# Which operand stays in TensorE in a compression of keys and values

## The reference

```
flat = blocks + pe                      # [n_cmp, 2 groups, 32 * 64]
k_cmp = gelu(flat @ w1) @ w2            # w1: 2048 x 256, w2: 256 x 64
k_cmp = rope(k_cmp at the block's end)  # keys only
```

## Time and profile before

| | |
|---|---|
| median of three timed runs | 3112.48 us |
| profiled execution | 3098.76 us, span 3097.4 us |
| TensorE matmul busy | 2260.3 us, 73% |
| TensorE weight load busy | 1385.4 us, 45% |
| VectorE busy | 1795.0 us, 58% |
| ScalarE busy | 462.6 us, 15% |
| GpSimd busy | 1330.2 us, 43% |
| DMA | 829.56 MB, 268 GB/s on average |
| mean granted TensorE clock | 0.802 of 2.4 GHz |

### The profile page before, as it was taken

How to read it: one execution, slowest core, us unless ns; L and a number is a source line. 1 busy time by engine, 2 the same in 40 slices (tenths; PEclk the granted TensorE clock), 3 DMA queues, 4 the chain that set the end, 5 groups by cost and what they waited for, 6 DMA issues and landing times. The chain is left out here.

```text
span 3097.4 us, 24710 instructions
## 1 busy us (share of the span) xinstructions
PE 2260.3 (73%) x8222; PEld 1385.4 (45%) x8222; DVE 1795.0 (58%) x3876; ACT 462.6 (15%) x1305; POOL 1330.2 (43%) x1041
## 2 busy tenths in 40 slices
PE   5997982046692594777684578979957687969988
PEld 3545861023442472533343336758425343437543
DVE  1512017988878777777567996774656954223300
ACT  1201000001210100111100332012000321013310
POOL 0000001376767677666668763674665533100000
PEclk9886996568695696898785557989977699986999
DMA  3310431589889899978889876999998879942466
GB/s 124 131 63 33 150 114 57 172 301 389 311 302 355 308 402 369 376 291 319 327 285 389 310 258 229 391 374 400 359 367 328 281 259 392 343 148 90 147 248 223
DMA packets 291758, 829.56 MB, mean 268 GB/s; under 512 B 23568, under 2 KB 30016, under 8 KB 290864
## 3 DMA queue, kind: packets, MB, share of 16 engines
q0 software_dynamic: 148464, 539.99, 47.8%
q1 hardware_dynamic: 139872, 283.19, 25.3%
q10 hardware_dynamic: 3296, 4.80, 0.4%
HBM read 825.81 MB, written 2.10 MB: 267 GB/s over the span
## 5 line engine op out<-in xcount | busy, mean ns | idle before, releaser
L314 POOL DMA_INDIRECT picks_rows<-peer_u_dram,expert x512 | 701.8, 1371 | 858.9 <-DVE expert L1475 521.0
L314 POOL DMA_INDIRECT picks_rows<-peer_v_dram,expert x512 | 620.8, 1213 | 502.8 <-DVE h L380 346.5
L374 DVE CUSTOM_DVE_ANT_0 picks_rows<-picks_rows,xn 128x1024 f32<-128x1024 f32 x512 | 613.4, 1223 | 168.7 <-DMA picks_rows<-peer_u_dram,expert 148.7
L380 DVE SCALAR_TENSOR_TENSOR h<-picks_rows,picks_weight,h 128x1024 f32<-128x1024 f32 x416 | 533.4, 1282 | 153.5 <-DMA picks_rows<-peer_v_dram,expert 82.8
L465 PE MATMUL psum<-weight_ring,hnT 128*128 128x512 f32 (+4 forms) x576 | 236.4, 572 | 23.9 <-DMA weight_ring<-w_in_dram 11.9
L1763 PE MATMUL psum<-weight_ring,aT 128*128 128x512 f32 x512 | 220.8, 593 | 2.9 <-ACT aT L2070 1.4
L403 PE MATMUL psum<-picks_rows,picks_diag 128*128 128x512 f32 x384 | 172.0, 607 | 27.4 <-ACT picks_diag L332 24.3
L465 PEld LDWEIGHTS psum<-weight_ring,hnT 128*128 128x128 f32 (+1 forms) x576 | 105.8, 186 | 153.1 <-issue 137.4
L656 PE MATMUL psum<-identity_sb,n_scaled 128*128 128x128 f32 (+1 forms) x104 | 23.9, 409 | 183.6 <-DVE n_scaled L640 183.6
L1763 PEld LDWEIGHTS psum<-weight_ring,aT 128*128 128x128 f32 x512 | 97.0, 190 | 125.1 <-issue 120.5
L876 PE MATMUL psum<-identity_sb,na_probs 128*128 128x128 f32 (+2 forms) x384 | 92.5, 360 | 72.3 <-DVE na_probs L962 56.2
(11 more groups left out here) (353 smaller groups left out, 3193.4 us busy)
## 6 DMA issues: line engine op xcount, KB each, us to landing
weight_ring<-w_ff_dram SPq DMA_DIRECT2D x48, 2048.0 KB, 10.9
weight_ring<-w_in_dram SPq DMA_DIRECT2D x44, 2048.0 KB, 14.2
weight_ring<-w_proj_nsa_dram SPq DMA_DIRECT2D x6, 2048.0 KB, 8.5
weight_ring<-w_out_dram SPq DMA_DIRECT2D x6, 2048.0 KB, 14.6
weight_ring<-w_ret_out_dram SPq DMA_DIRECT2D x4, 2048.0 KB, 7.8
weight_ring<-w_mix_out_dram SPq DMA_DIRECT2D x4, 2048.0 KB, 18.7
weight_ring<-w_peer_q_dram SPq DMA_DIRECT2D x4, 2048.0 KB, 13.4
picks_rows<-peer_u_dram,expert POOLq DMA_INDIRECT x512, 7.5
```

The source lines that it names most:

```text
L314: pool.indirect_dma_start(out=self.rows[:, n % GATHERS, :], out_offset=None, in_=table, in_offset=bass.IndirectOffsetOnAxis(ap=self.expert ...
L374: ins = nc.vector.tensor_tensor_reduce(out=row, in0=row, in1=self.x[t], scale=1.0, scalar=0.0, op0=ALU.mult, op1=ALU.add, accum_out=self.d ...
L380: ins = nc.vector.scalar_tensor_tensor(out=h, in0=row, scalar=self.weight[:, t % 2, k:k + 1], in1=h, op0=ALU.mult, op1=ALU.add)
```

## The change

`compress_stage` keeps the blocks in TensorE and moves the weights. For each l, all 32 columns of both groups (64 with a step of 16) are loaded, and the slab's 256 columns of that l move through. The result is 64 blocks by 256 hidden units in one bank, with one product group per slab. Gelu is applied to it (64x256). Two transposes then turn it, ScalarE copies the 128x128 that come out to `hidden`, and the w2 products follow as before. As all 32 columns are read in all runs, also those not yet written, a new stage clears `kc` once, right behind the table loads.

```
-        two += [("ck1", a["w_ck1"], 2), ("cv1", a["w_cv1"], 2)]
+        two += [("ck1", a["w_ck1"], 1), ("cv1", a["w_cv1"], 1)]
...
+    both = NG * S // CMP_STRIDE
...
-        hidden = sb("hidden", [P, 2, 2, NG * n])
+        by_block, hidden = sb("by_block", [both, 2, CMP_HID]), sb("hidden", [P, 2, 2, both])
...
+                blocks = kc[:, x].rearrange("p g (n l) -> p (g n) l", l=CMP_STRIDE)
+                for l in range(CMP_STRIDE):
+                    mm = nc.tensor.matmul(g.psum[0:both, 2 * x, 0:CMP_HID], blocks[:, :, l], w1[:, l, :], start=(l == 0),
+                                          stop=(l == CMP_STRIDE - 1))
+                mm.then_inc(g.w.products_done, 1)
+            for x in range(2):
+                pe.wait_ge(*s_hidden.after(x + 1))
                 for j in range(2):
-                    for l in range(CMP_STRIDE):
-                        rhs = kc[:, x, :, :].rearrange("p g (n l) -> p g n l", l=CMP_STRIDE)[:, :, 0:n, l]
-                        mm = nc.tensor.matmul(g.psum[:, 2 * x + j, 0:NG * n].rearrange("p (g n) -> p g n", g=NG),
-                                              w1[:, l, P * j:P * j + P], rhs, start=(l == 0), stop=(l == CMP_STRIDE - 1))
-                    mm.then_inc(g.w.products_done, 1)
-                    g.picks.add(pe, 2 * x + j + 1)
+                    mm = nc.tensor.transpose(g.psum[:, 2 * x + 1, both * j:both * j + both], by_block[:, x, P * j:P * j + P],
+                                             g.identity[0:both, 0:both])
+                mm.then_inc(s_flipped.sem, 1)
             for x in range(2):
-                pe.wait_ge(*s_hidden.after(2 * x + 2))
+                pe.wait_ge(*s_flat.after(x + 1))
                 for grp in range(NG):
                     for j in range(2):
                         mm = nc.tensor.matmul(g.psum[0:n, 4 + x, HD * grp:HD * grp + HD],
-                                              hidden[:, x, j, n * grp:n * grp + n], w2[:, x, j, :],
+                                              hidden[:, x, j, both // NG * grp:both // NG * grp + n], w2[:, x, j, :],
                                               start=(j == 0), stop=(j == 1))
...
-                for j in range(2):
-                    act.wait_ge(g.w.products_done, g.w.product(name, j))
-                    nc.scalar.activation(hidden[:, x, j, :], g.psum[:, 2 * x + j, 0:NG * n],
-                                         ACT.Gelu_apprx_tanh).then_inc(s_hidden.sem, 1)
+                act.wait_ge(g.w.products_done, g.w.product(name, 0))
+                nc.scalar.activation(by_block[:, x, :], g.psum[0:both, 2 * x, 0:CMP_HID], ACT.Gelu_apprx_tanh).then_inc(s_hidden.sem, 1)
                 g.picks.activate(act, 2 * x + 2)
+            for x in range(2):
+                act.wait_ge(*s_flipped.after(x + 1))
+                nc.scalar.copy(hidden[:, x].rearrange("p j n -> p (j n)"), g.psum[:, 2 * x + 1, 0:2 * both]).then_inc(s_flat.sem, 1)
...
+def clear_stage(g, name, tensor):
+
+    signal = g.named(name)
+    g.open(None, 1)
+    g.begin(g.nc.vector)
+    g.nc.vector.memset(tensor, 0.0).then_inc(signal.sem, 1)
+    signal.count += 1
+    g.ended["dve"] = signal.after(0)
...
+            clear_stage(g, "blocks_cleared", kc[:])
```

More of the change, by code:

```diff
@@ L1552, in compress_stage @@
     nc = g.nc
+    both = NG * S // CMP_STRIDE
     sig = lambda name: g.named(f"compress_{name}")
-    s_hidden, s_out, s_link, s_roped, s_turned = (sig(x) for x in ("hidden", "out", "link", "roped", "turned"))
+    s_hidden, s_flipped, s_flat, s_out, s_link, s_roped, s_turned = (
+        sig(x) for x in ("hidden", "flipped", "flat", "out", "link", "roped", "turned"))
     names = [("ck1", "second", run), ("cv1", "second", run)]
@@ L1623, in compress_stage @@
         vector(nc.vector)
-    s_hidden.count += 4
+    for signal in (s_hidden, s_flipped, s_flat):
+        signal.count += 2
     s_out.count += 2
@@ L1627, in compress_stage @@
     s_turned.count += 1
-    g.ended["pe"], g.ended["act"], g.ended["dve"] = s_turned.after(0), s_hidden.after(0), s_link.after(0)
+    g.ended["pe"], g.ended["act"], g.ended["dve"] = s_turned.after(0), s_flat.after(0), s_link.after(0)
 def pool_stage(g, tag, uT, tokens, inv_count, w_pool, pool_scale, ypT):
```

## The result

| | before | after |
|---|---|---|
| median | 3106.73 us (22 runs, 3093.57 to 3132.85 and one of 3519.11, which the ratio leaves out) | 3088.01 us (22 runs, 3073.15 to 3111.05) |
| ratio after/before | | 0.9942, 95% interval 0.9926 to 0.9958 |
| profiled execution | 3098.76 us, span 3097.4 | 3074.43 us, span 3073.1 |
| mean granted clock | 0.802 | 0.817 |

The kernel got 0.4 to 0.7% faster. The forecast of 3101.9 us was 13.9 us too high, and the range (from 3089) missed the time by 1 us. Repeated later, the changed kernel gave ratios of 0.9967 and 0.9969.

A forecast was written before the change was run, and what follows sets the result against it. Of three second-wave compression stages (runs 0, 1, 2), only run 2 was taken as bound by TensorE's narrow, low-clock products. Its stage gains 10.6 us (26.5 to 15.9), other parts 0: 3112.5 - 10.6 = 3101.9 us, range 3089 to 3113.

The forecast's parts named there:

- part 6: Turns and attention behind run 2's stage: clock falls in the tail, 0 gained; 8.5 us if it held.
- the base of the sum: Timed median before taken as 3112.5 us, 13.7 above the profiled execution; less 10.6 gives 3101.9.
- What bounds the kernel: Second wave's compression: TensorE carries run 2 (token tile 3), 26.47 us to VectorE's copy; other work ends runs 0 and 1.
- part 4: Runs 0 and 1: TensorE saves some 11 us in each but waits longer for picks; gain 0, upper bound 0.5.
- part 3: Compression slabs given back after one product group, with 1.6 us of cover in run 2; cost 0, upper bound 3.2 us.
- part 1: Run 2's first products: 64 records of 256 columns at 0.2155 us, 13.8 us against 25.34; upper bound 0.31 a record.
- (b): Run 2's products: strided weight load not hidden, 0.263 to 0.31 us a record, gain 4.5 to 7.6, about 3106.5; chance 0.09.
- (c): Run 2's products: 64 weight columns lose the clock, 0.427 us a record, 3.3 us slower, 3115.8; chance 0.06.
- part 2: Behind run 2's products: gelu wait and transposes add 1.0 us; stage 15.9 us against 26.5, gain 10.6; bounds 0.6 and 2.0.
- part 5: Clear behind the last selection: 128x2048 VectorE memset of 2.2 us, off the path, cost 0; without cover 2.3 us.
- signs that the prediction named: Run 2's following turns: clock 0.50 under the forecast, 1.00 under rival (a); also product pace and VectorE's copy at 16 us.
- rival (a): Clock holds through run 2's tail: 10.6 + 8.5 = 19.1 us gained, 3093.4; chance 0.27.

The follow-up runs named there:

- 124 columns side by side: Kernel before, with run 2's (token tile 3) products each moving 124 adjacent columns, wrong blocks; 128 records in 14.5 us, 296.2 us to the end.
- fillers: Changed kernel plus unread identity products in TensorE's waits in run 2 (token tile 3): 3077.70 and 3091.03 us, ratios 0.9929 and 0.9961 to before.
- 124 at the step: Kernel before, run 2 moving 124 columns at a 64-byte step: 62 read twice (3095.60 us, ratio 0.9991) or 124 different (310.3 us to the end).
- with the clear: Kernel before with only the clear of kc added: 3109.04 us, ratio 1.0002 to before.
- with run 2 as before: Kernel before with the clear and the new compression in runs 0 and 1 only, the old one in run 2: 3110.02 us, ratio 1.0007.
- side by side: Kernel before, with run 2's products each moving 62 adjacent columns, wrong blocks; 128 records in 25.4 us, 309.7 us to the end.

## Why the prediction was wrong

Two steps failed: the clock behind the stage, put at no gain (part 6), and the base of the sum, taken from three runs. The stage itself was forecast rightly.

*What bounds the kernel; runs 0 and 1 (part 4); slabs (part 3).* Right. Run 2 alone pays, with 86.2 and 48.3 us against 85.4 and 48.5 in the others. In run 2 no DMA ended a wait of the products: loads and matmuls have one idle gap each, ahead of the first.

```profile
L1576 PE MATMUL psum<-weight_ring,kc_sb x64: 379/379/454, 2776.7 to 2790.4; 128*64 128x256 f32 x64
its engine sat idle before it (us, times) until:
  ACT branch_gates L500: 1.1, 1
  DVE nsa_kv_sb L746: 1.0, 1
```

*First products (part 1).* Right: (14.05 - 0.38)/63 = 0.217 us a record against 0.2155. Rivals (b) and (c) are out; the strided load is hidden, and 64 weight columns hold the clock. The sentence of the Trainium skill (TensorE: Matmul & The Clock Gate, "Part 3: Packing small matmuls", "The mechanism"), by which the load would add to each record, gave 0.263: the trace contradicts it, and so do the 124 columns side by side, at 0.111 us with a load of 128 columns through all rows. The estimate that a record of the old stage takes 0.20 us at a clock of 0.50 counted the records at both ends of the window: it is 0.213, so its half is 0.107 and not 0.10, which moves only the upper bound. That this time is the weight load's, as the prediction put it, no run shows.

*What the change adds (part 2).* 0.3 us less than put: 15.56 us to VectorE's copy where 15.9 was forecast. So 10.9 us for the stage, not 10.6. The gain is again the clock's: the first w2 products and the signal took 0.77 us (2791.53 to 2792.30), where the prediction had 1.13 "as before", that is at 0.50.

*The clear (part 5).* Right in the sum, 0; the memset took 1.76 us, not 2.2.

*The clock behind the stage (part 6).* This step of the mechanism failed, in size. "A fall in the tail" was right, but "with 0 gained" was not: I took the clock as either held all along or lost with nothing won. It fell only at 2796, so behind VectorE's copy the turns of the keys and of q (0.42 us against 0.64, and 1.07 against 1.94) ran at 2.4 GHz, 1.1 us in all with their waits (34.44 - 26.47 = 7.97 us before, 22.44 - 15.56 = 6.88 now). It also came back 2 us sooner in attention, which gave 0.9 us by the third product with the compressed keys. Another 0.4 us lie more than 165 us behind the first product, where the clock stood at 0.50 from 180 to 190 us in before and at 0.68 from 170 to 180 us in the changed kernel; what they come from was not tested. 10.9 + 1.1 + 0.9 + 0.4 = 13.3, against 10.6. Of the signs that the prediction named, the turn of q showed that of rival (a), 1.00, and the turn of the keys and values behind it that of the forecast, 0.50. Rival (a), the clock held, was 8.5 us. Held by fillers it gave 0.4 us in the w2 products, 2.0 in the turns and 5.0 in attention up to the fourth product with the compressed keys, 7.3 us together before rounding; the later fall (see the clock in the tail) took 1.7 of them again.

*The sum.* This step was off by more than the mechanism: "The timed median is 13.7 us above that execution, and the difference carries over: 3112.5". That median was of three runs, and 22 runs gave 3106.73, so 5.7 us of the miss were in the base. With the right base and step it would have been 3106.7 - 13.3 = 3093.4. The remaining 5.4 us are what this median and the traces disagree on; no run gives them a cause, and the two repeats (15.3 and 10.3 us under their own before) stand on either side of 13.3. The lower end of the range was rival (a) with an allowance for the median; it had no room for a base that is too high beside a gain that is too small. So the 13.9 us are 5.7 of the base, 2.7 of the step and 5.4 (rounded) that stay open; by the two steps alone the time would have lain within the range.

## What to carry to other kernels

Split the path into the stretch that the change touches and the rest, and read the effect there as a difference of starts: here that is good to about a microsecond where medians of 12 runs are good to 8. For an fp32 product with few moving columns ask three things apart: whether it keeps the clock, whether the columns or a fixed time of each record set the pace, and whether the columns lie side by side. If the clock changes inside a stage, read the pace on both sides of the change first: here that alone gave 0.11 and 0.213 us for the same record. And take a pace from two starts, not from the count of a short window. And the base of a forecast of 0.3% deserves as much care as its terms; three runs are not enough of a median for it.

## What the runs showed of the hardware

- Moving fp32 columns 64 bytes apart go at about half rate: 0.212 us a record of 124 (1.7 ns a column) against 0.111 side by side, both at a clock of 1.00. At 0.50 the record at the step took the same 0.21. With 62 columns a record nothing of that is seen.
- A record with a load of 128 columns took no less than 0.11 us at a clock of 1.00 (62 and 124 columns) and 0.213 at 0.50 (30, 46 and 62 columns), whatever the step of the 62.
- As weights the 64-byte step is free behind 256 moving columns: 0.217 us a record.
- Products of 256 columns and of 124 side by side kept the clock of 1.00. With 62 columns it fell for the rest of the stage 2.1 to 2.7 us after the first product, in all five executions looked at (before twice, with the clear, with run 2 as before, and side by side). With 124 at the step it fell 2.1 to 2.4 us after the first product as well, but came back among the same products (at 2787.6 and 2790.9). Filler products of some 1 us in the waits kept it through transposes and the start of attention.
- A VectorE memset of 128x2048 fp32 takes 1.76 us.
- The spread of this kernel, 20 us and more, arises ahead of run 2, where the gathers are: up to there the executions lie 27 us apart (2776.7 to 2804.2), and behind it kernels with the same run 2 lie within 0.2 us of each other, but for one at 0.9, which lost the clock once more.
